# Decays of the delta rule and its first two units inside the last HGRN head

## The chip, the cores and the metric

One core of a Trainium2 chip runs the whole program. The metric is the time of one execution on the device in microseconds, the median of several runs. The core has a matrix engine (TensorE, PE in the rows), three others that work on tiles of 128 partitions (VectorE is DVE, ScalarE is ACT, GpSimd is POOL) and SyncE (SP), whose queue issues the loads of weights. PSUM has eight banks of 128x512 float32; `ps[:, b, :]` is bank b. The engines run their own instruction streams and wait for each other by semaphores only (`sig(name)`).

## The reference, cut to what matters

Two transformer blocks follow each other over 512 tokens of width 1024. The change lies in the mixer of the second, between its two recurrences (HGRN with 8 heads, then the gated delta rule with 8 pairs of value heads):

```python
proj = (u @ w_in).astype(f32)
(hq, hf, hi, hg, gq, gk, gv, ga, gb, gz, gate_h, gate_g) = jnp.split(proj, offsets, axis=-1)
...
o_h = hgrn2_chunked(to_chunks(q_h, HG_HEADS), to_chunks(k_h, HG_HEADS),
                    to_chunks(hi, HG_HEADS), to_chunks(log_f, HG_HEADS))
o_h = rmsnorm_2(from_chunks(o_h), hgrn_out_norm) * jax.nn.silu(hg).reshape(B, S, HG_HEADS, HG_DV)
...
qkv = jax.nn.silu(causal_short_conv(jnp.concatenate([gq, gk, gv], axis=-1), conv_w))
cq, ck, cv = jnp.split(qkv, [GDN_WIDTH_K, 2 * GDN_WIDTH_K], axis=-1)
...
beta = jax.nn.sigmoid(gb)
g = -jnp.exp(a_log.astype(f32)) * jax.nn.softplus(ga + dt_bias)
o_g = gated_delta_chunked(...)   # S_t = a_t (I - beta_t k_t k_t^T) S_{t-1} + beta_t k_t v_t^T, a_t = exp(g_t)
```

`ga` and `gb` are 16 columns of the projection each; from them come the decays (a running sum of `g`) and `beta`.

## The kernel before

**Units.** A weight matrix is worked through in units of 1024x128. SyncE loads a unit (512 KB) into one of four ring slots; ScalarE rounds it in two halves (`round_unit`, L438, about 0.6 us a half), GpSimd computes what the rounding left off (`split_unit`, L447), and TensorE makes 24 matmuls of 128x512 of it, three for each of eight tiles (`hi*hi`, `lo*hi`, `hi*lo`; L465 to L467, L1865 to L1867 in HGRN, L2346 to L2348 in the delta rule). ScalarE and GpSimd run two units ahead; `round_unit(u)` waits until unit u-2 has been multiplied, since there is room for four rounded halves. Four units make an HGRN head (F, Q, V, G). `ab_unit` holds the columns of `ga` and `gb` and comes behind the last of them, and the units of the delta rule follow: (0,0) and (0,1) are q and k of its head 0, (0,2) and (0,3) its two value heads.

**HGRN.** Each of the eight heads goes through seven level products (l = 0 to 6, L1938): VectorE makes differences (L2144, L2145), ScalarE their exponential (L2044), VectorE multiplies (L2164, L2165), TensorE makes four matmuls, VectorE gathers the result (L2172). Between the products of head h stand the late steps of head h-1 and units of head h+1. The late steps of a head are keys (transposes L1884, copied by ScalarE L1972), changes (L1898), states on VectorE (L2082, L2086), outputs (L1907, L1912), square and copy on ScalarE (L1978, L1979), sum (L1919), root (L1983), and on VectorE reciprocal (L2091) and gated output (L2096, L2099; signal `hg_out`). In the last head, numbered 7, no further HGRN head follows: only `ab_unit` stands between its products, and its own late steps come behind them.

**The delta rule's start.** Behind head 7 `act_load_gdn` loads two vectors of 16 numbers. `act_decays` (L2271 to L2289) and `dve_decays` (L2291 to L2307) read `ab_unit`'s bank and pass the work to and fro on 16 partitions: sigmoid, absolute value, exponentials, logarithm on ScalarE, sums and a scan on VectorE. `pe_decays` turns the rows (L2270), ScalarE copies them and takes an exponential, `pe_gd_rows` (L2327) spreads two rows over all partitions. Then TensorE works on units (0,0), (0,1), (0,2), makes the first sums (L2361) and unit (0,3), and the inverse products (L2371). VectorE takes differences (L2707), `dve_gd_conv` a convolution with four taps for each unit (L2734, three times L2736), ScalarE evacuates a unit (`act_gd_evac`, L2550) and then rounds another one. The bank of `ab_unit` is bank 1, which unit (0,1) uses next; bank 0 goes from Q to unit (0,0) and then to unit (0,2). The order on each engine is written out by hand.

## Time and profile before

| what | us |
|---|---|
| median of 3 runs | 3383.93 |
| lowest, highest | 3383.03, 3387.18 |
| the profiled execution | 3391.74 |
| its span, first to last instruction | 3389.9 |
| TensorE busy in the span | 3216.2 (95%) |
| VectorE, ScalarE, GpSimd busy | 1580.0, 1419.1, 1585.7 |
| mean granted clock of TensorE | 0.97 |

The profile is of one execution; its times count from the start of the span. A duration in its rows is that of an instruction or of a group of merged ones. Matmuls overlap each other, so the distance of two starts tells more than a duration. In brackets stands how long the engine had been idle before it and what released it; an x16 of matmul records stands for eight matmuls, as matmuls outside the units leave two each. A granted clock of 1.00 is 2.4 GHz, 0.50 is 1.2 GHz.

### The profile page before, as it was taken

Reading aid. Unit: us, or ns where it says so; the run is one execution under the profiler, and the core shown is the slowest. Engines: PE = TensorE matmul, PEld = TensorE weight load, DVE = VectorE, ACT = ScalarE, POOL = GpSimd, SP = SyncE. Lnnn points to the kernel's source line nnn. Section 1 sums busy time; section 2 is a strip of 40 time slices with the busy share of each in tenths; the row PEclk is TensorE's granted clock in tenths of the full one; section 3 lists DMA queues with packets and bytes.
Section 4 is the critical chain, followed back from the end, with each engine's and each line's share of the span. In section 5 each row is a group of like instructions: output and inputs, shape, how many; then the busy total and the mean of one; then the engine's idle time right before and its main releaser. Section 6 shows DMA issues by size and latency. Waiting matters only on the chain.

```text
span 3389.9 us, 44791 instructions
## 1 busy us (share of the span) xinstructions
PE 3216.2 (95%) x16754; PEld 2650.5 (78%) x16754; DVE 1580.0 (47%) x2189; ACT 1419.1 (42%) x2479; POOL 1585.7 (47%) x1361
## 2 busy tenths in 40 slices
PE   5889999999999999999989886999999999999998
PEld 4567888877788887888867775888888888888887
DVE  4783443146533322443077774555565652233321
ACT  3355333226743333333255544544554432243332
POOL 4345444665554456445542222444444434564454
PEclk8989999999999999999999987999999999999999
DMA  4212333341033333333322210111111123333332
GB/s 120 56 38 63 96 96 95 98 126 45 2 93 99 94 97 89 99 93 95 97 64 55 56 44 25 38 38 38 38 38 38 38 56 95 98 93 99 93 94 81
DMA packets 471621, 246.86 MB, mean 73 GB/s; under 512 B 13883, under 2 KB 468774, under 8 KB 471334
## 3 DMA queue, kind: packets, MB, share of 16 engines
q1 hardware_dynamic: 470144, 241.33, 25.2%
...
q14 instruction: 53, 0.43, 0.0%
...
## 4 chain that ended last, share of the span: by engine, by line
PE 86%; DVE 7%; ACT 3%; issue 3%; POOL 1%; DMA 0%; POOLq 0%; ACTq 0%; DVEq 0%
PE ps L465 19%; PE ps L466 19%; PE ps L467 19%; PE ps L2450 2%; PE ps L2346 2%; PE ps L2347 2%; PE ps L2348 2%; PE ps L2432 2%; PE ps L1645 2%; PE ps L1669 2%; PE ps L1655 2%; PE ps L1865 1%; PE ps L1938 1%; PE ps L1866 1%; PE ps L1867 1%
## 5 line engine op out<-in xcount | busy, mean ns | idle before, releaser
L447 POOL TENSOR_TENSOR w_lo<-ring,w_hi 128x512 fp32r<-128x512 f32 (+1 forms) x908 | 1225.8, 1372 | 1544.7 <-ACT w_hi L438 1544.6
L438 ACT ACTIVATE w_hi<-ring 128x512 fp32r<-128x512 f32 (+1 forms) x908 | 516.6, 618 | 1286.4 <-PE ps L467 1206.7
L465 PE MATMUL ps<-h_hi,w_hi 128*128 128x512 f32 x1776 | 702.0, 395 | 5.1 <-POOL w_lo L447 4.4
L467 PE MATMUL ps<-h_hi,w_lo 128*128 128x512 f32 x1776 | 692.8, 390 | 0.0
L466 PE MATMUL ps<-h_lo,w_hi 128*128 128x512 f32 x1640 | 640.0, 390 | 0.0
L465 PEld LDWEIGHTS ps<-h_hi,w_hi 128*128 128x128 f32 x1776 | 334.4, 188 | 82.2 <-POOL w_lo L447 6.4
L467 PEld LDWEIGHTS ps<-h_hi,w_lo 128*128 128x128 f32 x1776 | 334.3, 188 | 70.1
L466 PEld LDWEIGHTS ps<-h_lo,w_hi 128*128 128x128 f32 x1640 | 308.8, 188 | 68.1 <-issue 4.6
L466 PE MATMUL ps<-a_lo,w_hi 128*128 128x512 f32 x752 | 292.6, 389 | 0.0
L465 PE MATMUL ps<-a_hi,w_hi 128*128 128x512 f32 x720 | 280.8, 390 | 0.0
L467 PE MATMUL ps<-a_hi,w_lo 128*128 128x512 f32 x720 | 280.2, 389 | 0.0
L820 DVE TENSOR_TENSOR silu_g<-ps,silu_g 128x512 f32<-128x512 f32 x88 | 60.9, 692 | 394.8 <-PE ps L467 394.0
L833 DVE TENSOR_TENSOR rt<-ps,rinv 128x512 f32<-128x512 f32 x32 | 22.1, 692 | 385.7 <-PE ps L467 385.7
L2684 POOL TENSOR_TENSOR arena<-arena,cst 128x512 f32<-128x512 f32 x112 | 136.7, 1241 | 91.1 <-PE ps L2432 44.7
L2346 PE MATMUL ps<-h_hi,w_hi 128*128 128x512 f32 x384 | 171.3, 446 | 0.0
L466 PEld LDWEIGHTS ps<-a_lo,w_hi 128*128 128x128 f32 x752 | 141.2, 188 | 29.0
L467 PEld LDWEIGHTS ps<-a_hi,w_lo 128*128 128x128 f32 x720 | 135.1, 188 | 28.3
L465 PEld LDWEIGHTS ps<-a_hi,w_hi 128*128 128x128 f32 x720 | 135.2, 188 | 27.9
L2348 PE MATMUL ps<-h_hi,w_lo 128*128 128x512 f32 x384 | 155.6, 405 | 0.0
L2806 DVE TENSOR_TENSOR arena<-arena,ps 128x512 f32<-128x512 f32 x96 | 65.2, 687 | 168.5 <-PE ps L2450 168.5
L825 DVE TENSOR_TENSOR a_lo<-silu_g,a_hi 128x512 f32 x88 | 138.2, 1570 | 10.8
L1788 POOL TENSOR_SCALAR arena<-arena 128x256 f32<-128x256 f32 (+3 forms) x176 | 96.9, 567 | 88.8 <-DVE arena L1733 88.8
...
## 6 DMA issues: line engine op xcount, KB each, us to landing
...
```

Of the source, the lines that this page charges most:

```text
L438: act.activation(w_hi[:, (halves(u) + j) % PIECES, 0:n, :], slot(u)[:, j * n:(j + 1) * n, :], ACT.Copy) \
L447: pool.tensor_tensor(w_lo[:, q % PIECES, 0:n, :], slot(u)[:, j * n:(j + 1) * n, :], w_hi[:, q % PIECES, 0:n, :].bitcast(f32), ALU.subtract ...
L465: pe.matmul(dst, wh, hi(k), start=first and k == 0, stop=False)
L466: pe.matmul(dst, wh, lo(k), start=False, stop=False)
L467: ins = pe.matmul(dst, wl, hi(k), start=False, stop=last and k == 2 * n - 1)
L825: dve.tensor_tensor(a_lo[:, tile, :], silu_g[:, j, :], a_hi[:, tile, :].bitcast(f32), ALU.subtract) \
L1645: ins = pe.matmul(ps[:, score_banks(i), s * w:(s + 1) * w][:, hh, :], u["q"][rows_], u["k"][rows_], start=True, stop=True)
L1655: ins = pe.transpose(ps[:, 2 + hh, at:at + P], p_buf[:, p_slot(e), at:at + P][:, hh, :], ident)
L1788: ins = pool.tensor_scalar(x, x, row_inv[:, column], 1.0 if u["gate"] is None else u["gate"], ALU.mult, ALU.mult)
L2346: pe.matmul(bank, wh, h_hi[:, k, :], start=k == 0, stop=False)
L2348: ins = pe.matmul(bank, wl, h_hi[:, k, :], start=False, stop=k == KT - 1)
L2684: pool.tensor_tensor(tiles(ml[:, hh, :]), tiles(mm[:, hh, :]), spread(level[:, l, :], NT, P), ALU.mult) \
```

## The change

The loading of the two vectors and the clearing of `rows` move to the start of HGRN. ScalarE copies the 64 used rows of `ab_unit` into `ab_rows` (`act_ab_rows`), in a part of memory that HGRN does not use, and the decays read that copy. Unit (0,0) is made in two halves behind level products 1 and 2 of head 7 of HGRN; the second half starts behind product 2. Unit (0,1) is made between head 7's changes and outputs. ScalarE's decays stand between head 7's keys and its square, VectorE's between head 7's states and its reciprocal, the transposes behind head 7's sum. The roundings of units (0,2) and (0,3), which stood behind the evacuations of (0,0) and (0,1), stand at level 4 and behind head 7's copy.

```diff
--- before.py
+++ after.py
@@ -1964,8 +1964,20 @@
                     name, value = hg_evicted(h, HG_F)
                     pe.wait_ge(sig(name).sem, value)
                     unit_products(pe, ab_unit, ps[:, AB_BANK, :], lambda k: h_hi[:, k, :], m_lo_tile)
-        for step in (pe_hgrn_keys, pe_hgrn_changes, pe_hgrn_outputs, pe_hgrn_sum):
-            step(pe, HG_HEADS - 1)
+                elif not more and l == 1:
+
+                    name, value = hg_evicted(h, HG_Q)
+                    pe.wait_ge(sig(name).sem, value)
+                    pe_gd_quarters(pe, 0, 0, 0, 1)
+                elif not more and l == 2:
+                    pe_gd_quarters(pe, 0, 0, 2, 3)
+        pe_hgrn_keys(pe, HG_HEADS - 1)
+        pe_hgrn_changes(pe, HG_HEADS - 1)
+        pe.wait_ge(sig("ab_copied").sem, 1)
+        pe_gd_unit(pe, 0, 1)
+        pe_hgrn_outputs(pe, HG_HEADS - 1)
+        pe_hgrn_sum(pe, HG_HEADS - 1)
+        pe_decays(pe)
 
     def act_hgrn_keys(act, h):
         act.wait_ge(sig("keys_turned").sem, h + 1)
@@ -2023,6 +2035,7 @@
 
     def act_hgrn(act):
         act.wait_ge(sig("lb_diff").sem, 1)
+        act_load_gdn(act)
         act.activation(lb, lb_diff, ACT.Sigmoid).then_inc(sig("lb_ready").sem, 1)
         act.activation(one_lb, lb_diff, ACT.Sigmoid, scale=-1.0).then_inc(sig("lb_ready").sem, 1)
         round_unit(act, hg_unit(0, HG_V))
@@ -2052,11 +2065,12 @@
                     act_hgrn_turned(act, h)
                 elif l == 2:
                     round_unit(act, hg_unit(h + 1, HG_V) if more else gd_units + 1)
+                    if not more:
+                        act_ab_rows(act)
                 elif l == 4:
                     if h:
                         act_hgrn_outputs(act, h - 1)
-                    if more:
-                        round_unit(act, hg_unit(h + 1, HG_G))
+                    round_unit(act, hg_unit(h + 1, HG_G) if more else gd_units + 2)
             act.activation(h_eb, hb[:, h % 2, :], ACT.Exp).then_inc(sig("hg_eb").sem, 1)
             if h:
                 act_hgrn_root(act, h - 1)
@@ -2067,8 +2081,12 @@
                 act_hgrn_query(act, h + 1)
                 act_hgrn_log(act, h + 1)
                 round_unit(act, hg_unit(h + 2, HG_F))
-        for step in (act_hgrn_keys, act_hgrn_outputs, act_hgrn_root):
-            step(act, HG_HEADS - 1)
+        act_hgrn_keys(act, HG_HEADS - 1)
+        act_decays(act)
+        act_hgrn_outputs(act, HG_HEADS - 1)
+        round_unit(act, gd_units + 3)
+        act_hgrn_root(act, HG_HEADS - 1)
+        act_columns(act)
 
     def pool_hgrn(pool):
         for u in range(hg_units, gd_units):
@@ -2121,6 +2139,7 @@
         dve.wait_ge(x_ready.sem, after_ffn1)
         dve.tensor_tensor(lb_diff, gain[:, g0:g0 + HG_HEADS], gain[:, g0 + HG_HEADS:g0 + 2 * HG_HEADS], ALU.subtract) \
            .then_inc(sig("lb_diff").sem, 1)
+        dve.memset(rows[0:64, :], 0.0).then_inc(sig("rows_clear").sem, 1)
         dve.memset(ql, 0.0)
         dve.memset(kl, 0.0)
         ch.link(dve.memset(h_att, 0.0))
@@ -2197,6 +2216,7 @@
                 differences(h + 1, 0)
         dve_hgrn_out(dve, ch, HG_HEADS - 2)
         dve_hgrn_states(dve, HG_HEADS - 1)
+        dve_decays(dve, ch)
         dve_hgrn_inverse(dve, ch, HG_HEADS - 1)
         dve_hgrn_out(dve, ch, HG_HEADS - 1)
 
@@ -2218,7 +2238,7 @@
     row_col = area.take(NT, 64)
     neg_eg = area.take(NT, GD_V)
     to_end = area.take(2, NT)
-    g_abs, g_log, g_pos = mm[:, 0, :], mm[:, 1, :], uu[:, 0, :]
+    ab_rows, g_abs = k_end[:, 0, :], k_end[:, 1, :]
     small = area.take(4)
     root8, inv8 = area.take(2 * NT), area.take(2 * NT)
     o_sq = gd_x[:, :, 3:3 + T]
@@ -2259,7 +2279,6 @@
                 load(h, j)
 
     def act_load_gdn(act):
-        act.wait_ge(sig("hg_out").sem, HG_HEADS)
         for j, name in enumerate(("gdn_dt_bias_2", "gdn_a_log_2")):
             act.dma_start(small[0:GD_V, j:j + 1], a[name].rearrange("l v -> v l")).then_inc(sig("small_loaded").sem, 16)
 
@@ -2270,39 +2289,46 @@
             ins = pe.transpose(ps[:, 3, i * 64:(i + 1) * 64], rows[0:64, i * P:(i + 1) * P], ident[0:64, 0:64])
         ins.then_inc(sig("rows_turned").sem, 1)
 
+    def act_ab_rows(act):
+        act.wait_ge(unit_done.sem, ab_unit + 1)
+        act.activation(ab_rows[0:64, :], ps[0:64, AB_BANK, :], ACT.Copy).then_inc(sig("ab_copied").sem, 1)
+
     def act_decays(act):
-        ga, dt = ps[0:GD_V, AB_BANK, :], small[0:GD_V, 0:1]
         act.wait_ge(sig("small_loaded").sem, 32)
-        act.wait_ge(unit_done.sem, ab_unit + 1)
+        act.wait_ge(sig("ab_copied").sem, 1)
         act.wait_ge(sig("rows_clear").sem, 1)
-        act.activation(rows[32:32 + GD_V, :], ps[32:32 + GD_V, AB_BANK, :], ACT.Sigmoid).then_inc(sig("beta_ready").sem, 1)
-
-        act.activation(g_abs[0:GD_V, :], ga, ACT.Abs, bias=dt).then_inc(sig("gd_scalar").sem, 1)
+        act.activation(rows[32:32 + GD_V, :], ab_rows[32:32 + GD_V, :], ACT.Sigmoid).then_inc(sig("beta_ready").sem, 1)
+        act.activation(g_abs[0:GD_V, :], ab_rows[0:GD_V, :], ACT.Abs, bias=small[0:GD_V, 0:1]) \
+           .then_inc(sig("gd_scalar").sem, 1)
         act.wait_ge(sig("gd_scalar").sem, 1)
-        act.activation(g_abs[0:GD_V, :], g_abs[0:GD_V, :], ACT.Exp, scale=-1.0)
-        act.activation(small[0:GD_V, 2:3], small[0:GD_V, 1:2], ACT.Exp).then_inc(sig("gd_scalar").sem, 1)
+        act.activation(small[0:GD_V, 2:3], small[0:GD_V, 1:2], ACT.Exp)
+        act.activation(g_abs[0:GD_V, :], g_abs[0:GD_V, :], ACT.Exp, scale=-1.0).then_inc(sig("gd_scalar").sem, 1)
         act.wait_ge(sig("gd_scalar").sem, 2)
-        act.activation(g_log[0:GD_V, :], g_abs[0:GD_V, :], ACT.Ln, bias=ones[0:GD_V, 0:1]).then_inc(sig("gd_scalar").sem, 1)
+        act.activation(g_abs[0:GD_V, :], g_abs[0:GD_V, :], ACT.Ln, bias=ones[0:GD_V, 0:1]).then_inc(sig("gd_scalar").sem, 1)
+
+    def act_columns(act):
         act.wait_ge(sig("rows_turned").sem, 1)
         act.activation(row_col.rearrange("p i n -> p (i n)"), ps[:, 3, 0:NT * 64], ACT.Copy).then_inc(sig("gd_scalar").sem, 1)
         act.wait_ge(sig("gd_scalar").sem, 4)
         act.activation(neg_eg, row_col[:, :, 0:GD_V], ACT.Exp).then_inc(sig("gd_scalar").sem, 1)
 
     def dve_decays(dve, ch):
-        dve.wait_ge(sig("hg_out").sem, HG_HEADS)
-        dve.memset(gd_x[:, :, 0:3], 0.0)
-        dve.memset(rows[0:64, :], 0.0).then_inc(sig("rows_clear").sem, 1)
+        g = ab_rows[0:GD_V, :]
         dve.wait_ge(sig("small_loaded").sem, 32)
         dve.wait_ge(sig("gd_scalar").sem, 1)
-        ch.link(dve.tensor_scalar(g_pos[0:GD_V, :], ps[0:GD_V, AB_BANK, :], small[0:GD_V, 0:1], 0.0, ALU.add, ALU.max))
+        ch.link(dve.tensor_scalar(g, g, small[0:GD_V, 0:1], 0.0, ALU.add, ALU.max))
         dve.wait_ge(sig("gd_scalar").sem, 3)
-        ch.link(dve.tensor_tensor(g_pos[0:GD_V, :], g_pos[0:GD_V, :], g_log[0:GD_V, :], ALU.add))
-        ch.link(dve.tensor_scalar(g_pos[0:GD_V, :], g_pos[0:GD_V, :], small[0:GD_V, 2:3], -1.0, ALU.mult, ALU.mult))
+        ch.link(dve.tensor_tensor(g, g, g_abs[0:GD_V, :], ALU.add))
+        ch.link(dve.tensor_scalar(g, g, small[0:GD_V, 2:3], -1.0, ALU.mult, ALU.mult))
         dve.wait_ge(sig("rows_clear").sem, 1)
         for i in range(NT):
             tok = slice(i * P, (i + 1) * P)
-            ins = dve.tensor_tensor_scan(rows[0:GD_V, tok], ones[0:GD_V, :], g_pos[0:GD_V, tok], 0.0, ALU.mult, ALU.add)
+            ins = dve.tensor_tensor_scan(rows[0:GD_V, tok], ones[0:GD_V, :], g[:, tok], 0.0, ALU.mult, ALU.add)
         ins.then_inc(sig("rows_ready").sem, 1)
+
+    def dve_columns(dve, ch):
+        dve.wait_ge(sig("hg_out").sem, HG_HEADS)
+        dve.memset(gd_x[:, :, 0:3], 0.0)
         dve.wait_ge(sig("gd_scalar").sem, 5)
         ch.link(dve.tensor_scalar(neg_eg, neg_eg, -1.0, None, ALU.mult))
 
@@ -2320,6 +2346,8 @@
         if g:
             pe.wait_ge(sig("gd_qkl").sem, 2 * g)
             pe.wait_ge(sig("keys_tok").sem, HG_HEADS + g)
+        else:
+            pe.wait_ge(sig("roots").sem, HG_HEADS)
         if g >= 2:
             pe.wait_ge(sig("gd_o_root").sem, 2 * (g - 1))
         for hh in range(2):
@@ -2510,10 +2538,7 @@
         pe_gd_quarters(pe, h, 5, 2, 3)
 
     def pe_gdn(pe):
-        pe_decays(pe)
         pe_gd_rows(pe, 0)
-        pe_gd_unit(pe, 0, 0)
-        pe_gd_unit(pe, 0, 1)
         pe_gd_unit(pe, 0, 2)
         pe_gd_sums(pe, 0)
         pe_gd_unit(pe, 0, 3)
@@ -2546,11 +2571,12 @@
             if 4 * h + j >= 2:
                 act.wait_ge(sig("gd_conv").sem, 4 * h + j - 1)
             else:
-                act.wait_ge(sig("rows_clear").sem, 1)
+                act.wait_ge(sig("hg_out").sem, HG_HEADS)
             act.activation(gd_x[:, j % 2, 3:3 + T], unit_bank(h, j), ACT.Copy).then_inc(sig("gd_evac").sem, 1)
         else:
             act.activation(gd_og(h, j - 4), unit_bank(h, j), ACT.Silu).then_inc(sig("gd_gate").sem, 1)
-        round_unit(act, gd_unit(h, j) + AHEAD)
+        if h or j >= 2:
+            round_unit(act, gd_unit(h, j) + AHEAD)
 
     def act_gd_silu(act, g, j):
         act.wait_ge(sig("gd_conv").sem, 4 * g + j + 1)
@@ -2643,7 +2669,6 @@
             act.activation(gd_o_sb(h)[:, hh, :], ps[:, 4 + hh, :], ACT.Copy).then_inc(sig("gd_o").sem, 1)
 
     def act_gdn(act):
-        act_decays(act)
         act_gd_eg(act, 0)
         act_gd_decay(act, 0)
         for j in range(2):
@@ -2858,7 +2883,7 @@
                     dve_gd_first(dve, g)
 
     def dve_gdn(dve, ch):
-        dve_decays(dve, ch)
+        dve_columns(dve, ch)
         dve_gd_diff(dve, 0)
         dve_gd_decay(dve, ch, 0)
         for j in range(3):
@@ -3104,7 +3129,6 @@
             act_ffn(act, plans["ffn1"], plans["mid"], plans["mix_norm"])
             act_norm(act, plans["mix_norm"])
             act_hgrn(act)
-            act_load_gdn(act)
             act_gdn(act)
             act_branches(act)
             act_out(act, plans["mix_out"], plans["ffn2_norm"])
```

**TensorE, last head, around its level products 1 to 3.** L1938 is a level product, L1898 the changes of head 6, L1907 its outputs. Before:

```order
L1938 MATMUL ps<-arena 128x128 [waits hg_att,hg_level]
L1938 MATMUL ps<-arena 128x128 x3
L1898 MATMUL ps<-arena 128x128 [waits hg_o,hg_hv,keys_tok]
L1898 MATMUL ps<-arena 128x128 x6
L1938 MATMUL ps<-arena 128x128 [waits hg_att,hg_level]
```

Now, where L2374 to L2376 are unit (0,0), 12 matmuls in each half:

```order
L1898 MATMUL ps<-arena 128x128 [waits hg_o,hg_hv,keys_tok]
L1898 MATMUL ps<-arena 128x128 x6
L2374 MATMUL ps<-h_hi,w_hi 128x512 [waits half_split,hg_evac]
L2375 MATMUL ps<-m_lo_tables,w_hi 128x512
L2376 MATMUL ps<-h_hi,w_lo 128x512
...
L1938 MATMUL ps<-arena 128x128 [waits hg_att,hg_level]
L1938 MATMUL ps<-arena 128x128 x3
L2374 MATMUL ps<-h_hi,w_hi 128x512 [waits half_split]
L2375 MATMUL ps<-m_lo_middle,w_hi 128x512
```

A half of the unit stands ahead of product 2 and one ahead of product 3. Unit (0,1) is inserted in the same way behind the second row of L1898 of head 7, and its first matmul waits for `half_split` and `ab_copied`.

**ScalarE, end of the last head.** L1972 and L1984 are the copy of head 7's keys, L1978 and L1990 its square. Before:

```order
L1972 ACTIVATE arena<-ps 128x512 [waits keys_turned]
L1978 ACTIVATE arena<-ps 128x512 [waits hg_out,hg_out_done]
L1979 ACTIVATE arena<-ps 128x512
L1983 ACT_TABLE_LOAD
L1983 ACTIVATE rt<-ps,eps_col 128x512 [waits head_sum]
```

Now:

```order
L1984 ACTIVATE arena<-ps 128x512 [waits keys_turned]
L2300 ACT_TABLE_LOAD [waits rows_clear,ab_copied]
L2300 ACTIVATE arena<-arena 16x512 [waits small_loaded]
L2301 ACTIVATE arena<-arena 16x512
L2304 ACT_TABLE_LOAD
L2304 ACTIVATE arena<-arena 16x1 [waits gd_scalar]
L2305 ACTIVATE arena<-arena 16x512
L2307 ACT_TABLE_LOAD
L2307 ACTIVATE arena<-arena,cst 16x512 [waits gd_scalar]
L1990 ACTIVATE arena<-ps 128x512 [waits hg_out,hg_out_done]
L1991 ACTIVATE arena<-ps 128x512
L438 ACTIVATE w_hi<-ring 128x512 [waits unit_done,unit_loaded1]
```

Three table loads and five activations stand ahead of the square, a rounding ahead of the root.

**VectorE, end of the last head.** L2086 and L2104 are the states of head 7, L2091 and L2109 its reciprocal. Before:

```order
L2086 SCALAR_TENSOR_TENSOR arena<-arena,ps 128x128 [waits states] x6
L2091 RECIPROCAL rinv<-rt 128x512 [waits roots]
L2096 SCALAR_TENSOR_TENSOR arena<-arena,gain,rinv 128x512 [waits roots,vector_chain]
L2099 TENSOR_TENSOR arena<-arena 128x512 [waits hg_evac,vector_chain]
L2293 MEMSET arena 128x2x3 [waits hg_out]
```

Now:

```order
L2104 SCALAR_TENSOR_TENSOR arena<-arena,ps 128x128 [waits states] x6
L2319 TENSOR_SCALAR arena<-arena 16x512 [waits gd_scalar,small_loaded]
L2321 TENSOR_TENSOR arena<-arena 16x512 [waits gd_scalar,vector_chain]
L2322 TENSOR_SCALAR arena<-arena 16x512 [waits vector_chain]
L2326 SCALAR_TENSOR_TENSOR arena<-cst,arena 16x128 [waits rows_clear,vector_chain]
L2326 SCALAR_TENSOR_TENSOR arena<-cst,arena 16x128 x3
L2109 RECIPROCAL rinv<-rt 128x512 [waits roots]
```

The sums and the scan now precede the reciprocal.

## Rows read from the trace of the kernel before

**Rows 1.** The page: chain that ended last, shares by engine

```profile
PE 86%; DVE 7%; ACT 3%; issue 3%; POOL 1%; DMA 0%; POOLq 0%; ACTq 0%; DVEq 0%
```

**Rows 2.** Waits of TensorE, 2026 to 2081: total us, times, longest

```profile
PE ps L2270 <- DVE arena L2304: 16.0, 1, 16.0
```

**Rows 3.** The chain in order of time, 2040 to 2056: start, us, what

```profile
2040.74 3.37 DVE rinv L2091
...
2044.92 0.70 DVE arena L2099
...
2046.57 1.28 ACT L2278
...
2053.33 0.69 DVE arena L2299
...
2054.56 1.37 DVE arena L2304 x4
```

**Rows 4.** Timeline of TensorE, last head: start, us, line, operation, [idle before]

```profile
2006.27 1.16 PE L1898 MATMUL ps<-arena 64*128 64x128 f32 x14
...
2011.45 2.08 PE L1938 MATMUL ps<-arena 128*128 128x128 f32 x8 [2.94 <-DVE arena L2165]
...
2021.31 1.95 PE L1938 MATMUL ps<-arena 128*128 128x128 f32 x16
...
2025.24 1.16 PE L1898 MATMUL ps<-arena 64*128 64x128 f32 x14 [0.82 <-ACT arena L1972]
2032.30 0.77 PE L1907 MATMUL ps<-arena 128*128 128x128 f32 x2 [5.90 <-issue]
```

**Rows 5.** Timeline of TensorE, head 6

```profile
1975.01 1.05 PE L1938 MATMUL ps<-arena 128*128 128x128 f32 x8
...
1983.19 3.40 PE L1938 MATMUL ps<-arena 128*128 128x128 f32 x16 [2.91 <-DVE arena L2165]
```

**Rows 6.** Windows of 2 us, TensorE: window, length, busy, granted clock, DMA, GB/s

```profile
2064.00:2066.00 2.00, 2.00 (x7) 0.61 0.00 0
...
2106.00:2108.00 2.00, 2.00 (x15) 0.87 0.01 4
```

**Rows 7.** The chain through unit (0,0), one matmul of 128x512 each

```profile
2063.22 0.43 PE ps L2346
...
2066.43 0.23 PE ps L2346
```

**Rows 8.** Timeline of ScalarE at the start of HGRN

```profile
1720.81 1.15 ACT L438 ACTIVATE w_hi<-ring 128x512 fp32r<-128x512 f32 x2 [3.32 <-PE ps L1867]
```

**Rows 9.** Timeline of ScalarE, head 6: square of head 5, rounding

```profile
1978.50 0.60 ACT L1978 ACTIVATE arena<-ps 128x512 f32<-128x512 f32 x1 [6.39 <-PE ps L1912]
...
1979.47 1.15 ACT L438 ACTIVATE w_hi<-ring 128x512 fp32r<-128x512 f32 x2
```

**Rows 10.** Timeline of VectorE: states of head 7

```profile
2029.93 2.26 DVE L2086 SCALAR_TENSOR_TENSOR arena<-arena,ps 128x128 f32<-128x128 f32 x6
```

**Rows 11.** Timeline of ScalarE: square and root of head 7

```profile
2037.26 0.60 ACT L1978 ACTIVATE arena<-ps 128x512 f32<-128x512 f32 x1 [12.07 <-PE ps L1912]
...
2040.02 0.69 ACT L1983 ACTIVATE rt<-ps,eps_col 128x512 f32<-128x512 f32 x1 [0.38 <-PE ps L1919]
```

**Rows 12.** Timeline of TensorE: first sums, inverse products behind unit (0,3)

```profile
2080.81 1.92 PE L2361 MATMUL ps<-cst,arena 128*128 128x1 f32 x16 [1.45 <-ACT arena L2564]
...
2089.76 1.95 PE L2371 MATMUL ps<-cst,arena 128*128 128x128 f32 x16
```

**Rows 13.** Timelines of VectorE (three taps twice, eight differences) and of GpSimd (split)

```profile
2069.67 4.37 DVE L2736 SCALAR_TENSOR_TENSOR arena<-arena,conv_w 128x512 f32<-128x512 f32 x3
...
2093.97 2.33 DVE L2736 SCALAR_TENSOR_TENSOR arena<-arena,conv_w 128x512 f32<-128x512 f32 x3
...
2121.74 2.16 DVE L2707 TENSOR_SCALAR arena<-ps,arena 128x128 f32<-128x128 f32 x8
...
2069.71 2.99 POOL L447 TENSOR_TENSOR w_lo<-ring,w_hi 128x512 fp32r<-128x512 f32 x2 [60.95 <-ACT w_hi L438]
```

## The prediction

> **What bounds the kernel now.** First the chain of the page [rows 1]: 86% of the span hangs on TensorE, so what can be won is time in which TensorE stands still or runs slowly for others. Then the waits of TensorE between the last HGRN head and the first delta-rule head [rows 2]: one gap of 16.0 us. The chain through it [rows 3] reads: reciprocal on VectorE at 2040.74, gated output of head 7 ended at 2045.62, small ScalarE steps of the decays from 2046.57 until VectorE's sum at 2053.33, the scan to 2055.93. None of this needs TensorE before the four transposes. TensorE's other gaps in the last head are the 2.94 us ahead of its level products at 2011.45 and 5.90 us ahead of the outputs at 2032.30 [rows 4]. And it is slow there: eight matmul records of a level take 2.08 us at 2011.45 and 1.05 us in head 6 at 1975.01 [rows 4, 5]. These are the clock's levels of 1.2 and 2.4 GHz; the granted clock rises to 2.4 only within 2064:2066, some 9 us after TensorE resumed, and in 2106:2108, 6 us after it resumed at 2100 [rows 6]. A unit is 24 matmuls, so 24 x 0.43 = 10.3 us at the low level and 24 x 0.23 = 5.45 us at the high one [rows 7].
>
> **The start of HGRN: nothing.** Two small DMAs (0.8 us of ScalarE's queue between 2045.64 and 2046.57, from [rows 3]) and a memset of 0.5 us move ahead of head 0. They and a table load of 1.28 us that now stands behind the wait shift ScalarE's next roundings by at most 1.9 us. ScalarE idles 3.32 us there until TensorE finishes a unit at 1720.81 [rows 8], which hides it. Without that cover it costs up to 1.9 us.
>
> **The last head, levels.** TensorE gets unit (0,0) in two halves, around level product 2. Its weights are there: the rounding and split of both first units are done at this point in the kernel before too. From the state changes at 2006.27 (1.1 us) [rows 4]: half a unit 2.72, product 0.9, half a unit 2.72, so product 3 comes at 2013.7 instead of 2011.45. But it no longer stands idle for 2.94 us, so I take the high clock from here on. That is what head 6 did: it also had unit work here. So head 6 is the template, shifted by 2013.7 - 1975.0 = 38.7 us: its products of levels 5 and 6 at 1983.19 [rows 5] give 2021.9, against 2021.31: +0.6. The template includes ScalarE's rounding of 1.15 us at 1979.47 [rows 9], which head 7 now has too. The template's 16 products took 3.40 us, head 7's 1.95 [rows 4, 5], since the clock had dropped; half of that stands before the last gather, so VectorE is 0.6 + 0.7 = 1.3 us late, and TensorE's changes start at about 2026.6 instead of 2025.24 (+1.4). The copy of the 64 rows (0.6 us on ScalarE) falls where ScalarE is early and costs nothing; at most 0.6.
>
> **The last head, tail.** Changes end at 2027.7; unit (0,1) takes 5.45, to 2033.2. VectorE's states, which ended at 2032.19 [rows 10], end at 2033.45. So the unit fills the old 5.90 us gap and outputs start at 2033.6, +1.3. If the unit ran at the low clock it would end at 2038.0. TensorE has now worked on, so the outputs go at the template's speed: 2.6 us (product 3 at 1975.01, 0.9 later the outputs, ScalarE's square at 1978.50 [rows 5, 9]) instead of 2032.30 to 2037.26 [rows 4, 11]. The square starts at 2036.2, -1.1. ScalarE's decays need 2046.57 to 2053.24, 6.7 us [rows 3], from the keys' copy at 2026.55, so to 2033.2: hidden under unit (0,1) and the outputs with 3 us to spare. VectorE's part, 3.3 us with the scan, runs 2033.5 to 2036.8, before the root that its reciprocal waits for. ScalarE then has square and copy 1.0, a rounding 1.05 and a table load 1.28: root at 2039.55 instead of 2040.02 [rows 11], -0.5. The output of head 7 ends at 2045.15 instead of 2045.62.
>
> The trace's table loads are 1.28 us, and the next ScalarE step follows at once: 2046.57 to 2053.24 holds three of them and all the steps. The Trainium skill (ScalarE: Activation LUTs, What ACT_TABLE_LOAD costs) puts a switch at 2.66 us with a drain of 1.38 us. By it the three moved ones would add 4.1 us, ScalarE would be 1.2 us late for the square, and the sum would be 1.2 us smaller. The trace shows no such drain.
>
> **From there to the first sums.** Before, 2045.62 to 2080.81 [rows 3, 12], 35.2 us: decays, row products, units (0,0), (0,1), (0,2). Now, from 2045.15: small ops 0.3 us, VectorE's differences 2.16 (eight [rows 13]), exponential 0.65, evacuation 0.6 (128x512 copies [rows 11]) to 2048.85. Row products and transposes have run behind the sum of head 7 and the root (2040 to 2044), with VectorE still at the reciprocal. Two branches follow. VectorE's two convolutions: with POOL at work three taps cost 4.37 us, without it 2.33 [rows 13]; the splits that ran beside them have moved away, so 0.5 + 2.33 each: ready 2054.9, and with 1.33 of activations the sums could start at 2056.2. TensorE: unit (0,2) waits for the first evacuation of its bank, a new wait, with sums and unit (0,3) queued behind it. It starts after some 5 us of idleness, so at the low clock: between 5.45 and 10.3 us. The nearer rows are the restarts, 9 and 6 us of low clock [rows 6]; I take 9.2. So 2058.2, against 2080.81: **-22.6 us**.
>
> **Unit (0,3).** Sums and unit took 2080.81 to 2089.76, 8.95 us, since a gap of 1.45 us preceded and the clock fell [rows 12]. Now TensorE comes straight from a unit: 1.8 + 5.45 = 7.2, -1.7 (bounds 0 and -1.7; I take the latter, as head 6's clock held while TensorE ran without a gap). Behind 2089.76 each step waits for the same as before. Sum: **-24.3 us**. Bounds: unit (0,2) all at low clock and no gain in (0,3), -21.6; VectorE as limit, -26.3.
>
> On the profiled execution, 3391.74 (span 3389.9), this gives 3367.4. The median of the unprofiled runs is 3383.93, 7.8 lower with the same program, and the difference carries over: 3383.93 - 24.3 = **3359.6**.
>
> **Rivals.**
> (a) Low clock under unit (0,1). For it: idle gaps of 2.9 us ahead of the products of level 5 remain, and in head 6 the clock fell there. Against it: head 6 was back at the high level after 3.5 us. Price: 4.8 for the unit and some 2.1 for slow outputs and sum, 6.9: -17.4, 3366.5.
> (b) The convolutions stay at 4.9 us each, because POOL's new splits or others fall on them. Then sums at 2060.4, +2.2: -22.1, 3361.8. Against it: both splits are queued ahead, in the last head.
> (c) The decays are not hidden, and the change does not do what it says: if ScalarE came to head 7's keys more than 3 us late, every further us is paid, to 6.7 + 3.3 = 10.0 in full: -14.3, 3369.6. Against it: TensorE has to make the unit first.
> (d) Slower: TensorE falls to 1.2 GHz at 2011 as before and never recovers in this stretch, although it has more to do. Then both moved units cost 10.3: product 3 comes 8.3 us late, the rounding adds 1, unit (0,1) sets the outputs 14.9 us late, head 7 ends 15.5 late; of the 35.2 us 21 go, so -5.5 at the sums and -2.4 after (0,3). It decides from the point where the low level lasts through 9 us of work beyond 2106: 20 us of such work give +17.6, 3401.5. Against it: full granted clock in 2106:2108 after a much longer idle time.
>
> **How the numbers follow.** Chances: the forecast with its bounds 0.68, (b) 0.10, (a) 0.12, (c) 0.04, (d) 0.02; 0.04 for a larger part given back behind the first sums, to within 0.2%. The range reaches from -26.3 with about 2 us of run scatter (3383.03 to 3387.18 before) to (a) with the same: 3355.5 to 3368. About 0.2% (6.8 us) is what a measurement of this kernel can tell from no change. Faster: 0.68 + 0.10 + 0.12 + 0.04 = 0.94; same 0.04; slower 0.02.
>
> **What would show it.** Right: no 16 us wait before the transposes; the row of outputs (7) at half its old length, within 2 us of 2033.6; granted clock 1.00 over 2008 to 2018; convolution taps of 0.76 us; the sums 22 to 24 us earlier. Wrong: TensorE waits for the outputs or unit (0,1) at 0.43 us per matmul (a); root (7) later than 2041 with ScalarE as its releaser (c); a changed distance from inverse products to the end.

## The result, and the profile after

| | before | changed |
|---|---|---|
| median of 4 runs each | 3385.01 | 3362.64 |
| lowest, highest | 3383.03, 3387.18 | 3360.66, 3366.61 |
| the profiled execution | 3391.74 | 3363.93 |
| its span | 3389.9 | 3362.1 |
| TensorE busy | 3216.2 | 3206.2 |
| mean granted clock | 0.970 | 0.976 |

The ratio is 0.9936, with a 95% interval of 0.9922 to 0.9950: 22.4 us less. Two more comparisons of the same pair, on two chips, gave 24.7 and 22.8 us. The forecast was 3359.6, with a range of 3355.5 to 3368.0.

The waits of TensorE between 2000 and 2070 in the changed kernel (total us, times, longest):

```profile
PE ps L2374 <- ACT arena L2575: 4.7, 1, 4.7
PE ps L1938 <- DVE arena L2184: 2.9, 1, 2.9
PE ps L2355 <- ACT rt L1995: 2.0, 1, 2.0
```

The 16.0 us of [rows 2] are gone. What is late now is the evacuation of a bank, L2575, for unit (0,2). The timeline of TensorE (start, us, line, operation, idle before) answers [rows 4, 12]:

```profile
2004.41 1.16 PE L1898 MATMUL ps<-arena 64*128 64x128 f32 x14
...
2011.97 1.05 PE L1938 MATMUL ps<-arena 128*128 128x128 f32 x8
...
2020.15 3.33 PE L1938 MATMUL ps<-arena 128*128 128x128 f32 x16 [2.91 <-DVE arena L2184]
...
2024.96 1.16 PE L1898 MATMUL ps<-arena 64*128 64x128 f32 x14 [0.69 <-ACT arena L1984]
...
2031.70 0.46 PE L1907 MATMUL ps<-arena 128*128 128x128 f32 x2
...
2035.03 1.12 PE L1919 MATMUL ps<-arena,cst 128*128 128x512 f32 x2 [0.69 <-ACT arena L1990]
...
2038.55 3.78 PE L2355 MATMUL ps<-arena,cst 16*128 16x512 f32 x4 [2.00 <-ACT rt L1995]
2047.03 0.80 PE L2374 MATMUL ps<-h_hi,w_hi 128*128 128x512 f32 x1 [4.70 <-ACT arena L2575]
...
2054.66 1.84 PE L2389 MATMUL ps<-cst,arena 128*128 128x1 f32 x16
...
2061.93 1.95 PE L2399 MATMUL ps<-cst,arena 128*128 128x128 f32 x16
```

Executions reach this place at different times (2003.0 to 2008.5 us in the traces of this case), so I measure from the changes of head 6 (L1898, 2006.27 before, 2004.41 here). The forecast for each step follows from its own time less 2006.27:

| us from the changes of head 6 to | before | forecast | changed |
|---|---|---|---|
| level product 3 | 5.18 | 7.4 | 7.56 |
| products of levels 5 and 6 | 15.04 | 15.6 | 15.74 |
| outputs of head 7 | 26.03 | 27.3 | 27.29 |
| square of head 7 | 30.99 | 29.9 | 29.97 |
| root of head 7 | 33.75 | 33.3 | 33.40 |
| end of head 7's output | 39.35 | 38.9 | 38.99 |
| first sums L2361, now L2389 | 74.54 | 51.9 | 50.25 |
| inverse products L2371, now L2399 | 83.49 | 59.2 | 57.52 |

So the stretch became 26.0 us shorter. From the inverse products to the end it is 1300.14 us before and 1300.17 after: nothing is given back in these two traces. The spans differ by 27.8, and the other 1.9 us lie ahead of this stretch: 1.1 us before HGRN, where no instruction was changed (ScalarE's last instruction ahead of it starts at 1712.46 and 1711.37), and 0.8 us within HGRN.

Three more things that the prediction asked to be looked at. ScalarE, end of the last head:

```profile
2030.95 0.73 ACT L2307 ACTIVATE arena<-arena,cst 16x512 f32<-16x512 f32 x1
2034.38 0.60 ACT L1990 ACTIVATE arena<-ps 128x512 f32<-128x512 f32 x1 [2.70 <-PE ps L1912]
...
2037.81 0.69 ACT L1995 ACTIVATE rt<-ps,eps_col 128x512 f32<-128x512 f32 x1
...
2046.40 1.07 ACT L2575 ACTIVATE arena<-ps 128x512 f32<-128x512 f32 x2
```

The decays end at 2031.68, and ScalarE still waits 2.70 us for the outputs: they are hidden, with 2.7 us to spare (3 in the forecast). VectorE, the first two convolutions:

```profile
2047.86 2.33 DVE L2761 SCALAR_TENSOR_TENSOR arena<-arena,conv_w 128x512 f32<-128x512 f32 x3
...
2050.63 2.33 DVE L2761 SCALAR_TENSOR_TENSOR arena<-arena,conv_w 128x512 f32<-128x512 f32 x3
```

Three taps take 2.33 us, as without GpSimd [rows 13], so rival (b) did not happen. And windows of 2 us of the granted clock (length; busy time of PE, PEld, DVE, ACT, POOL; clock; DMA; GB/s):

```profile
2010.00:2012.00 2.00, 2.00 (x11) 1.65 (x10) 1.49 (x5) 0.00 (x0) 0.00 (x0) 1.00 0.12 35
...
2038.00:2040.00 2.00, 1.45 (x2) 0.83 (x3) 1.47 (x1) 1.98 (x3) 0.55 (x1) 0.50 0.13 26
...
2048.00:2050.00 2.00, 2.00 (x6) 1.56 (x5) 1.93 (x3) 0.77 (x1) 0.00 (x0) 0.50 0.00 0
2050.00:2052.00 2.00, 2.00 (x7) 1.56 (x7) 1.93 (x4) 0.63 (x1) 0.00 (x0) 0.65 0.00 0
2052.00:2054.00 2.00, 2.00 (x11) 1.61 (x10) 0.92 (x2) 1.01 (x2) 0.00 (x0) 1.00 0.00 0
```

With unit (0,0) between the levels the clock was full at 2010, as forecast. Unit (0,2) began at half clock, and the clock rose 4.4 us after its start: 7.63 us for the unit, where the forecast had 9.2. The clock had not fallen in the 4.70 us wait: it was at 0.50 in 2038:2040 already, under the row products at 2038.55, and stayed there through the wait.

### The profile page after: what moved, and what is told of

Its sections match the earlier page's. It is cut to its first block, busy times and chain, and to the rows that moved or that the text cites. A ratio compares the mean times of both kernels' runs of the same rounds, so it can differ in the third digit from the quotient of the medians.

```text
span 3362.1 us, 44794 instructions
## 1 busy us (share of the span) xinstructions
PE 3206.2 (95%) x16754; PEld 2644.2 (79%) x16754; DVE 1577.6 (47%) x2189; ACT 1418.8 (42%) x2480; POOL 1586.7 (47%) x1361
## 3 DMA queue, kind: packets, MB, share of 16 engines
q10 hardware_dynamic: 1318, 3.35, 0.3%
## 4 chain that ended last, share of the span: by engine, by line
PE 87%; DVE 7%; ACT 3%; issue 2%; POOL 1%; DMA 0%; POOLq 0%; DVEq 0%; ACTq 0%
PE ps L465 19%; PE ps L467 19%; PE ps L466 19%; PE ps L2478 2%; PE ps L2374 2%; PE ps L2376 2%; PE ps L2375 2%; PE ps L2460 2%; PE ps L1645 2%; PE ps L1669 2%; PE ps L1865 2%; PE ps L1938 2%; PE ps L1655 2%; PE ps L1866 2%; PE ps L1867 1%
## 5 line engine op out<-in xcount | busy, mean ns | idle before, releaser
L465 PEld LDWEIGHTS ps<-h_hi,w_hi 128*128 128x128 f32 x1776 | 334.0, 188 | 82.1 <-POOL w_lo L447 6.4
L466 PEld LDWEIGHTS ps<-h_lo,w_hi 128*128 128x128 f32 x1640 | 308.5, 188 | 67.9 <-issue 4.6
L2374 PE MATMUL ps<-h_hi,w_hi 128*128 128x512 f32 x384 | 170.8, 445 | 4.7 <-ACT arena L2575 4.7
L465 PEld LDWEIGHTS ps<-a_hi,w_hi 128*128 128x128 f32 x720 | 135.2, 188 | 27.8
L2376 PE MATMUL ps<-h_hi,w_lo 128*128 128x512 f32 x384 | 155.0, 404 | 0.0
L825 DVE TENSOR_TENSOR a_lo<-silu_g,a_hi 128x512 f32 x88 | 138.2, 1570 | 10.8
```

Source lines behind the costliest of these rows:

```text
L465: pe.matmul(dst, wh, hi(k), start=first and k == 0, stop=False)
L466: pe.matmul(dst, wh, lo(k), start=False, stop=False)
L825: dve.tensor_tensor(a_lo[:, tile, :], silu_g[:, j, :], a_hi[:, tile, :].bitcast(f32), ALU.subtract) \
L2374: pe.matmul(bank, wh, h_hi[:, k, :], start=k == 0, stop=False)
L2376: ins = pe.matmul(bank, wl, h_hi[:, k, :], start=False, stop=k == KT - 1)
```

## Experiments

Theory: the gain has two parts that hang together, the decays under head 7 and the two units in TensorE's gaps. ScalarE's loads cost 1.28 us and have 2.7 us to spare. Behind head 7 what ends last is VectorE's chain to the evacuation, then unit (0,2) at a low clock. Rivals: one of the two parts does all of it; table loads cost more than they show; the clock, not the waits, holds the gain. Distances are from the changes of head 6 unless said otherwise.

**The changed kernel again (after_again, after_third).**

> The changed kernel once more, for its own interval and a second trace. By the theory that the profiled pair's 27.8 us of span are 26.0 us from the last HGRN head to the inverse products and 1.9 us of chance before them, the median gain is 24 to 26 us, and the distance from the first product of level 1 in head 7 (2003.42 in the first trace) to the inverse products (2061.93) is again 58.5 us within 2. By the rival that the first runs' 22.4 us is the true gain and something gives 3 to 4 us back when no profile is taken, the median gain is 21 to 23 us.

> The changed kernel once more, as the neighbour of the next two on the same chip. Expected 24 us below the kernel before, and 57 to 58 us from the changes of head 6 to the inverse products, 67 to 69 us to the transposes L2414.

Measured in after_again: 3361.48 against 3386.19 (ratio 0.9927, 0.9913 to 0.9942), 57.53 us to the inverse products. In after_third: 3366.86 against 3389.70 (0.9937, 0.9923 to 0.9950), 56.75 us there and 67.1 to the transposes L2414. The local gain, always against the one trace of before, repeats as 26.0 and 26.7 us. The medians give 24.7, inside the 24 to 26 of the theory, and 22.8, inside the 21 to 23 of the rival, so they do not decide between the two.

**Each part alone.** decays_only takes the units back out of the last head; units_only puts the decays back behind it:

```diff
 # decays_only
-                elif not more and l == 1:
...
-                    pe_gd_quarters(pe, 0, 0, 0, 1)
-                elif not more and l == 2:
-                    pe_gd_quarters(pe, 0, 0, 2, 3)
...
-        pe_gd_unit(pe, 0, 1)
         pe_hgrn_outputs(pe, HG_HEADS - 1)
...
         pe_gd_rows(pe, 0)
+        pe_gd_unit(pe, 0, 0)
+        pe.wait_ge(sig("ab_copied").sem, 1)
+        pe_gd_unit(pe, 0, 1)
 # units_only
-        act_decays(act)
         act_hgrn_outputs(act, HG_HEADS - 1)
...
     def act_gdn(act):
+        act_decays(act)
```

(The roundings go back with the units, the transposes and VectorE's part with the decays.)

> Only the decays, the copy of their rows and the loading and clearing are moved; units (0,0) and (0,1) and the roundings stand where they stood before. Theory (the 16.0 us wait is the decays' own): the row products follow the root of head 7 directly, at 2040.6 of the old trace instead of 2056.65, and everything behind shifts with them: -16 us. VectorE is then at its reciprocal and output until 2045.6, under the two units. Rival (the decays' gain needs the units as cover for ScalarE's 6.7 us): ScalarE is late for head 7's square, -10 us or less.

> Only units (0,0) and (0,1) and their roundings are moved; the decays stand behind head 7's output as before, though they read the copy. Theory: the root of head 7 is 0.4 us early, the decays take their 10.3 us with TensorE idle, then rows, differences and evacuation to about 17 us behind the output, unit (0,2) 8 to 10 us: sums at about 2070.5 instead of 2080.8, -10 us. Together with the decays alone that is the whole gain, so the parts add. Rival (units moved ahead only fill gaps that the clock makes worth more: faster outputs and products): -13 us or more.

Measured: decays_only 3369.63 (0.9950, 0.9935 to 0.9965), 16.6 us less than before; units_only 3376.28 (0.9967, 0.9955 to 0.9979), 9.9 us less. TensorE's timeline, decays_only first, then units_only:

```profile
2027.18 0.77 PE L1907 MATMUL ps<-arena 128*128 128x128 f32 x2 [5.29 <-issue]
...
2035.64 2.92 PE L2346 MATMUL ps<-arena,cst 16*128 16x512 f32 x3 [0.16 <-ACT rt L1986]
```

```profile
2055.06 0.68 PE L2285 MATMUL ps<-cst,arena 64*128 64x64 f32 x4 [15.46 <-DVE arena L2322]
2055.67 3.77 PE L2351 MATMUL ps<-arena,cst 16*128 16x512 f32 x4
2062.45 0.79 PE L2370 MATMUL ps<-h_hi,w_hi 128*128 128x512 f32 x1 [3.00 <-ACT arena L2572]
```

Without the decays' move the 15.5 us wait stays, without the units' move the gap ahead of head 7's outputs stays. To the inverse products the parts save 17.1 and 13.5 us alone, 30.6, and 26.0 together. The windows of this stretch (columns as above: TensorE's busy time stands first, the granted clock behind GpSimd) tell what was saved, in the order before, decays_only, units_only, changed:

```profile
2006.27:2089.76 83.49, 55.20 (x241) 43.73 (x241) 45.64 (x74) 34.30 (x50) 11.44 (x8) 0.69 0.10 26
```

```profile
2003.24:2069.62 66.38, 53.26 (x242) 41.91 (x241) 44.62 (x73) 34.90 (x51) 11.42 (x8) 0.77 0.12 32
```

```profile
2007.40:2077.44 70.04, 46.88 (x241) 36.89 (x241) 41.83 (x73) 34.84 (x51) 10.66 (x8) 0.81 0.11 29
```

```profile
2004.41:2061.93 57.52, 46.53 (x241) 36.79 (x241) 41.62 (x73) 34.87 (x51) 10.67 (x8) 0.85 0.13 35
```

| us less than before | decays_only | units_only | changed |
|---|---|---|---|
| TensorE idle (length less busy time, 28.3 before) | 15.2 | 5.1 | 17.3 |
| TensorE busy with the same matmuls (55.2 before) | 1.9 | 8.3 | 8.7 |

So the last rival holds in part: a third of the local gain, 8.7 of 26.0 us, is the same work at a higher granted clock, and in these traces it comes with the units. (The other two traces of the changed kernel are busy for 46.5 and 43.3 us; before has one trace.) This is the mechanism of the rival in units_only's expectation, and its trace gives that rival's size (13.5 us), while its median gives the theory's (9.9).

Of the 4.6 us by which the parts' sum exceeds the whole, 3.0 are idle time and 1.6 busy time. TensorE waits for the evacuation ahead of unit (0,2) for 4.70 us in the changed kernel and 3.00 in units_only. In decays_only it does not wait there: VectorE's reciprocal and output of head 7 run while TensorE makes both units. That this new wait is the whole of the 3.0 us is not shown. By medians, on one chip, the parts give 16.6 and 9.9, which exceeds the whole (24.7) by 1.8 only. Either way neither part does it alone.

**What a table load costs (pad6, pad2).** Extra activations of one column behind the decays, each with another function than the last:

```diff
         act_decays(act)
+        for i in range(6):      # pad2: 2
+            act.activation(root8[0:GD_V, i:i + 1], small[0:GD_V, 0:1], (ACT.Exp, ACT.Sigmoid)[i % 2])
         act_hgrn_outputs(act, HG_HEADS - 1)
```

> The changed kernel with six small activations behind the moved decays on ScalarE, each with a table load of its own; they write scratch columns and change no result. Theory (the decays are hidden with 2.7 us to spare, what is above that is paid in full): six times 1.28 + 0.2 us, 8.9 us in all, so head 7's square comes 6.2 us late and the whole is 6 us longer. Rival by the page (ScalarE: Activation LUTs, What ACT_TABLE_LOAD costs, of the Trainium skill: 2.66 us for each switch): 16 us, the square 13 us late.

> The changed kernel with two extra activations of 1 column on 16 partitions behind ScalarE's decays, each with another function, so with a table load of its own. By the trace's loads (1.28 us, next activation at once) they add 2.9 us, against 2.7 us that ScalarE waited for the outputs of head 7: the square comes 0.3 us later and nothing else moves. By 2.66 us for a switch they would add 5.5 us, and the square would come 2.8 us later.

Timeline of ScalarE, pad6, then pad2:

```profile
2031.71 1.28 ACT L2087 ACT_TABLE_LOAD   x1
2033.00 0.20 ACT L2087 ACTIVATE arena<-arena 16x1 f32<-16x1 f32 x1
2033.21 1.28 ACT L2087 ACT_TABLE_LOAD   x1
...
2040.62 0.57 ACT L1990 ACTIVATE arena<-ps 128x512 f32<-128x512 f32 x1
```

```profile
2034.68 1.28 ACT L2087 ACT_TABLE_LOAD   x1
...
2037.48 0.20 ACT L2087 ACTIVATE arena<-arena 16x1 f32<-16x1 f32 x1
2038.96 0.60 ACT L1990 ACTIVATE arena<-ps 128x512 f32<-128x512 f32 x1 [1.28 <-PE ps L1912]
```

Six switches with their activations took from 2031.71 to 2040.62, 8.9 us, 1.49 each, and the square came 6.24 us later than in the changed kernel: 8.9 less the 2.7 to spare. From there every microsecond was paid: 64.00 us to the inverse products against 57.52. (The times, 3367.44 for pad6 and 3368.26 for pad2, are of one run each and cannot tell this.) Two took 3.0 us, as expected, but the square was not late: TensorE ran slowly in this execution (changes of head 7 2.07 us long, not 1.16), and ScalarE still waited 1.28 us for it. What there is to spare thus depends on the clock. By 2.66 us for a switch with its drain, which the Trainium skill gives (ScalarE: Activation LUTs, What ACT_TABLE_LOAD costs), six would by estimate have taken some 16 us. The runs show none of the drain: in pad6 a load ends 0.01 us before the activation behind it starts.

**What stands behind head 7 (round_late, warm, both).** round_late rounds unit (0,3) behind the root, not ahead of it. warm has TensorE multiply into an unused bank during the new wait. both is round_late with the evacuations and the convolutions ahead of the decay's exponentials and differences:

```diff
 # round_late
-        round_unit(act, gd_units + 3)
         act_hgrn_root(act, HG_HEADS - 1)
+        round_unit(act, gd_units + 3)
 # warm
         pe_gd_rows(pe, 0)
+        for _ in range(3):
+            pe.matmul(ps[:, 2, :], ones, mixT[:, 0, :], start=True, stop=True)
         pe_gd_unit(pe, 0, 2)
 # both, besides
         act_gd_eg(act, 0)
-        act_gd_decay(act, 0)
...
         act_gd_squares(act, 0)
+        act_gd_decay(act, 0)
...
+        for j in range(2):
+            dve_gd_conv(dve, ch, 0, j)
         dve_gd_diff(dve, 0)
```

> The changed kernel with one thing moved: the rounding of unit (0,3) stands behind head 7's root instead of ahead of it. Theory (that rounding, 1.05 us, is on the chain: the sum of head 7 is ready 0.4 us before ScalarE comes to the root): root, reciprocal and all behind come 1.0 us earlier than in the changed kernel, so the span from head 7's square to its root falls from 3.43 to 2.4 us. Rival: the split then falls on VectorE's reciprocal or output and stretches them by as much; no change.

> The changed kernel with three float32 matmuls of 128x512 behind the row products, into a bank that nobody reads: they add work and change no result. Theory (unit (0,2) is slow at its start because TensorE idles 4.7 us ahead of it): unit (0,2) now takes 5.5 us instead of 7.6, but the sums then wait for VectorE's convolutions and come only 0.3 to 0.4 us earlier. Rival (the granted clock falls for another reason): unit (0,2) takes 7 us or more again.

> The changed kernel with two things moved: the rounding of unit (0,3) behind head 7's root, and the two evacuations and convolutions of units (0,0) and (0,1) ahead of the differences and their exponentials. Theory (a new chain output of head 7, differences, exponentials, evacuation, unit (0,2) sets the time, of which differences and exponentials, 2.9 us, are not needed that early): 1.0 + 2.6 = 3.6 us less from head 6's changes to the inverse products, which was 57.5. Rival: VectorE becomes the limit and the gain is under 1.5 us.

| us | changed | round_late | warm | both |
|---|---|---|---|---|
| median | 3361.48 | 3362.09 | 3366.96 (one run) | 3361.81 |
| changes of head 6 to sum of head 7 (L1919) | 30.62 | 31.75 | 32.96 | 32.91 |
| sum of head 7 to first sums | 19.63 | 18.89 | 19.25 | 15.87 |
| changes of head 6 to inverse products | 57.52 | 57.91 | 59.52 | 56.92 |

The medians of the changed kernel and of round_late come from one chip (before 3386.19), those of the other two from another (before 3388.84). Behind the sum of head 7 each did about what was expected. In round_late the distance from this sum to the row products L2355 fell from 3.52 to 2.48, and 0.74 of it was left at the first sums. In both the first sums stand 3.8 us closer. In warm unit (0,2) began at the same distance from the sum of head 7 (12.01 us, 12.00 in the changed kernel) and ran in some 6.2 us instead of 7.63. Then TensorE waited for ScalarE's last activation ahead of the sums, which stands behind VectorE's second convolution, so only 0.4 us was left, as expected:

```profile
2060.75 1.92 PE L2389 MATMUL ps<-cst,arena 128*128 128x1 f32 x16 [0.90 <-ACT arena L2592]
```

Ahead of the sum of head 7, where these kernels have the changed kernel's order on every engine, TensorE lost 1.1 to 2.3 us more to the low clock (the changes of head 7 took 2.07 us instead of 1.16, and unit (0,1) began slowly). This is rival (a) in part: of the eleven executions with both parts of the change whose traces I have (the two pads among them), five took 30.2 to 30.6 us for this distance, three 31.75 and two 32.9 (the eleventh is pad6, which delays the square).

So the distance that the expectation of both named, from head 6's changes to the inverse products, fell by 0.6 us and not by 3.6, the size of its rival but not by its mechanism. The median of round_late shows no gain (24.1 us below before, the changed kernel 24.7 on the same chip). That of both is 27.0 us below before on its chip (0.9915, 0.9899 to 0.9930), an interval that overlaps those of the changed kernel.

**A bank of its own for unit (0,2) (rebank, rebank_again, rebank2).** Bank 2 is free there. So unit (0,2) need not wait for L2575, and unit (0,3) comes ahead of the sums. ScalarE evacuates units (0,2) and (0,3) earlier in its order, and VectorE's fourth convolution moves ahead of its work on q and k (not shown below), so this is more than one change:

```diff
 # rebank, besides the edits of both
-        return ps[:, gd_place[h, j] % 2, :]
+        return ps[:, 2 if (h, j) == (0, 2) else gd_place[h, j] % 2, :]
...
         pe_gd_unit(pe, 0, 2)
-        pe_gd_sums(pe, 0)
         pe_gd_unit(pe, 0, 3)
+        pe_gd_sums(pe, 0)
 # rebank2: the differences first again, the exponentials behind evacuations 0 and 1
         dve_gd_diff(dve, 0)
         for j in range(2):
             dve_gd_conv(dve, ch, 0, j)
...
         for j in range(2):
             act_gd_evac(act, 0, j)
+        act_gd_decay(act, 0)
```

> As the kernel with both moves, and unit (0,2) goes to bank 2, so that TensorE needs no evacuation for it; unit (0,3) follows it directly, ahead of the sums. Theory (the 4.7 us gap of TensorE is the new wait that the changed kernel paid for the old one): no gap ahead of unit (0,2), VectorE is the limit from head 7's output to the first products of the delta rule, and the distance from head 6's changes to the transposes there (67.9 in the changed kernel) is 4 to 5.5 us less. Rival: VectorE and GpSimd hold each other up and it is no shorter than in the kernel with both moves.

> The same kernel as rebank, to compare it with the changed kernel on one chip. If the gain seen there was its own: 8 us (5 to 10) below the changed kernel of the same chip. If most of it was the chip or chance: 2 us, what its trace shows up to the transposes L2414 (65.9 us from the changes of head 6, 67.9 in the changed kernel).

> As rebank, but VectorE's differences come back ahead of its first two convolutions and ScalarE's two exponentials L2564 ahead of its first Silu, so that no table load and no idle 2.75 us of VectorE stand between. Expected: the first sums at the same distance from the sum of head 7 (18.6 us), the wait ahead of the inverse products 2 us instead of 4.6, the transposes L2414 2 to 3 us earlier from the changes of head 6 (63 to 64 us), and the median 2 to 3 us below rebank. Rival: the third convolution now falls on GpSimd's split and stretches, and the gain is under 1 us.

TensorE of rebank, then of rebank2:

```profile
2036.47 1.12 PE L1919 MATMUL ps<-arena,cst 128*128 128x512 f32 x2 [0.69 <-ACT arena L1990]
...
2041.63 0.80 PE L2374 MATMUL ps<-h_hi,w_hi 128*128 128x512 f32 x1
...
2055.11 1.84 PE L2389 MATMUL ps<-cst,arena 128*128 128x1 f32 x16
2061.57 3.78 PE L2399 MATMUL ps<-cst,arena 128*128 128x128 f32 x16 [4.61 <-DVE arena L2769]
...
2072.20 1.97 PE L2414 MATMUL ps<-cst,arena 128*128 128x128 f32 x8 [3.99 <-DVE arena L2810]
```

```profile
2036.98 1.13 PE L1919 MATMUL ps<-arena,cst 128*128 128x512 f32 x2 [0.69 <-ACT arena L1990]
...
2060.76 3.52 PE L2399 MATMUL ps<-cst,arena 128*128 128x128 f32 x16 [3.34 <-DVE arena L2769]
...
2070.20 1.97 PE L2414 MATMUL ps<-cst,arena 128*128 128x128 f32 x8 [3.99 <-DVE arena L2810]
```

The wait ahead of unit (0,2) is gone, but 4.6 us of it came back ahead of the inverse products, where VectorE's convolutions and the norms are late, and the inverse products ran at 3.78 us instead of 1.95, at the low clock. From the sum of head 7 to the transposes L2414 the distances are 37.3, 37.4 and 37.0 us in the three traces of the changed kernel, 34.3 in both, 35.7 and 35.7 in rebank and rebank_again, 33.2 in rebank2. So rebank gains 1.5 us here and less than both: its rival (no shorter than both) came true. From the changes of head 6, as its expectation measured, it is 65.9 us and 67.4 in rebank_again against 67.9, not 4 to 5.5 less. rebank2 gains 4, the further 2.5 that were expected (63.4 us from the changes of head 6). Its wait fell to 3.34 and not to 2, as its third convolution ran beside a split of GpSimd (4.09 us for three taps). That is its rival's mechanism, but the gain over rebank was 2.5 us and not under 1.

The medians say otherwise: rebank 3353.42 against 3388.84 before (0.9897, 0.9882 to 0.9912), rebank_again 3356.60 against 3389.70 (0.9901, 0.9886 to 0.9916), and on this second chip the changed kernel 3366.86 and rebank2 3363.83 (0.9923, 0.9909 to 0.9938; lowest 3353.08, highest 3366.03). Rebank is 10.3 us better than the changed kernel on one chip with 1.5 us to show for it, and rebank2 is 7.2 us worse than rebank with a better stretch, where 2 to 3 us less was expected. The stretch measured so far does not hold the difference, so I looked behind it. VectorE runs one instruction (L2769, L2744 before) once for each head of the delta rule; its starts in rebank2:

```profile
2290.77 0.20 DVE L2769 RECIPROCAL arena<-arena 128x8 f32<-128x8 f32 x1
2372.81 0.20 DVE L2769 RECIPROCAL arena<-arena 128x8 f32<-128x8 f32 x1
2454.86 0.20 DVE L2769 RECIPROCAL arena<-arena 128x8 f32<-128x8 f32 x1
2540.09 0.20 DVE L2769 RECIPROCAL arena<-arena 128x8 f32<-128x8 f32 x1
```

Two heads take 82.05 us each and the third 85.23, with the same instructions. Two windows of 6 us of the quicker head from 2290.77, and the same two of the slower head from 2454.86, both of rebank2:

```profile
2332.77:2338.77 6.00, 6.00 (x42) 5.45 (x42) 4.66 (x11) 2.68 (x5) 0.00 (x0) 1.00 0.00 0
2356.77:2362.77 6.00, 6.00 (x43) 5.48 (x42) 5.82 (x9) 3.89 (x7) 3.00 (x3) 1.00 0.16 48
```

```profile
2496.86:2502.86 6.00, 6.00 (x33) 5.41 (x33) 3.97 (x11) 2.15 (x5) 0.00 (x0) 0.72 0.00 0
2520.86:2526.86 6.00, 5.59 (x28) 4.86 (x29) 5.82 (x10) 1.65 (x3) 2.09 (x3) 0.72 0.33 90
```

In the slower head the clock falls twice for part of such a window (0.72 on the mean, 1.00 in its other windows), where the windows just before had 0.25 and 1.81 us without matmuls. In the quicker head the windows at the same places had 0.25 and 2.22 us without, and the clock stays at 1.00. The seven distances between the heads, in order:

| kernel | us from one head to the next |
|---|---|
| before | 71.0, 83.5, 85.2, 85.2, 82.1, 85.2, 85.3 |
| changed | 69.3, 83.5, 85.2, 85.2, 82.1, 85.2, 85.3 |
| after_again | 67.7, 85.2, 85.2, 82.0, 85.2, 82.0, 85.2 |
| after_third | 69.0, 83.5, 85.1, 85.2, 85.2, 82.0, 85.2 |
| rebank | 67.7, 83.4, 85.1, 85.1, 85.2, 85.3, 82.1 |
| rebank_again | 67.2, 82.0, 82.1, 82.0, 85.3, 82.1, 85.2 |
| rebank2 | 66.1, 82.1, 82.1, 82.0, 82.1, 85.2, 85.2 |

Behind the inverse products rebank2 is 9.7 us shorter than the changed kernel (1290.5 against 1300.2). Of this 7.8 us are in the last six distances (498.7 against 506.5 in sum), where rebank2 has four of 82 us and the changed kernel one. The other 1.8 lie ahead of the second start of L2769. The profiled execution of rebank2 was its fastest run (four of its six took 3363.5 to 3366.0), that of rebank its slowest (3363.07), and its trace has one quick head only. Whether rebank's order makes the quicker heads more likely or met them by luck is open: its eight runs on two chips reach from 3351.9 to 3363.1, the changed kernel's fifteen in three comparisons from 3358.5 to 3369.9. That rebank is faster than the changed kernel is measured on one chip (four runs up to 3357.7, five from 3361.2 on). That its 10 us come from its edit is not shown.

## Why the prediction was right, point by point

- *Start of HGRN, nothing*: right. ScalarE's table load stands there at 1720.89 instead of 1721.98, early by the 1.1 us that this execution had ahead of HGRN. ScalarE's idle time ahead of its rounding is 2.12 us instead of the 3.32 of [rows 8], so 1.2 us were absorbed (at most 1.9 forecast).
- *The last head as head 6 shifted*: right to 0.2 us at each step of the table, including the rounding. The clock was at 1.00 in every window from 2008 to 2018, as forecast. Before it had been 0.74 in 2010:2012 and 0.50 from 2012 on.
- *The tail*: outputs +1.26 (forecast +1.3), square -1.0 (-1.1), root -0.35 (-0.5). The decays hidden under unit (0,1), with 2.7 us to spare; pad6 showed the cover by using it up. Rival (c) is thereby out.
- *To the first sums, -22.6*: -24.3 measured. The mis-sized term is unit (0,2): 7.63 us and not 9.2, inside its bounds of 5.45 to 10.3. I had sized it by two restarts at low clock of 9 and 6 us [rows 6], and this one rose after 4.4. Its start, 42.6 us from the changes of head 6, was exact, so the chain ahead of it (reciprocal, output, differences, exponential, evacuation) was read rightly, new wait included. A faster unit would have won almost nothing more, as the second branch of the forecast, VectorE's convolutions with ScalarE's activations, ended at 2054.67, with the unit (warm: 0.4 us).
- *Unit (0,3), -1.7*: sums and unit took 7.27 us (7.2 forecast, 8.95 before).
- *Sum*: -24.3 forecast, -26.0, -26.0 and -26.7 in three traces against the one trace of before, -22.4, -24.7 and -22.8 by medians. The forecast lay between, and the scatter of the medians, 2.3 us, is as large as the error. The prediction opened with waits and put the clock inside its terms. Of the 26.0 us in the trace 17.3 were waits and other idle time of TensorE, and 8.7 were the clock.
- *The predicted median* is 3.0 us below the measured one. 1.1 of it is the other kernel: before measured 3385.01 here, not 3383.93. The other 1.9 are the difference of 24.3 and 22.4. The step behind that is "the difference carries over": the profiled execution of before stood 6.7 us above its median of 3385.01, that of the changed kernel 1.3 above its own. Which part of before's 6.7 us lay in this stretch no trace tells.
- *Rivals*: (b), (c) and (d) did not occur. (a) occurs in part, as chance: five executions of ten lose 1.1 to 2.8 us between the changes of head 6 and the sum of head 7, and never the 6.9 of (a), since unit (0,1) begins slowly but does not stay slow.
